# Two blocks on one core: the first two projections interleaved with their splits moved off GpSimd, and the heads' spreads and the mixing weights' loads moved

## The reference

```python
h = concatenate([meta, x])                      # 16 + 1024 tokens, width 1024
u = rmsnorm(h, norm_g)
proj = u @ w_in                                 # 1024 -> 2304 columns
f_in, f_gate, q, k, v, a_gate = split(proj)     # 512, 512, 512, 128, 128, 512
f_out = fourier_branch(f_in, w_fmix, b_fmix) * silu(f_gate)
a_out = attention_branch(rope(rmsnorm(q)), rope(rmsnorm(k)), v) * silu(a_gate)
h = h + concatenate([f_out, a_out]) @ w_out
x = rmsnorm(h, final_g)[:, 16:]
# fourier_branch: real part of a 2D FFT over tokens and 64 channels of a group,
# then a 64 x 64 mix for each of 8 groups, plus b_fmix
... second block: retention and latent attention, gated feed-forward, gated embedding
```

## Time and profile before

| | us |
|---|---|
| median of 3 runs (2277.14 to 2283.83) | 2279.16 |
| the profiled execution | 2278.32 |
| its span | 2276.3 |
| TensorE busy, share of the span | 92% |
| first projection begins | 33.78 |
| projection of v ended | 113.1 |
| gate 7 ended | 290.7 |

### The profile page before, as it was taken

The page is one execution under the profiler, slowest core; times in us unless marked ns, Lnnn a source line. Parts: engine busy times, 40 slices in busy tenths (PEclk is TensorE's granted clock), DMA queues, the critical chain, the costliest instruction groups (busy, mean ns, idle before and its releaser), DMA issues.

```text
span 2276.3 us, 24686 instructions
## 1 busy us (share of the span) xinstructions
PE 2085.4 (92%) x9915; PEld 1718.9 (76%) x9915; DVE 1167.8 (51%) x1592; ACT 703.0 (31%) x1220; POOL 708.5 (31%) x460
## 2 busy tenths in 40 slices
PE   4988998999799999978888798999999999999878
PEld 3976866777687888856776586788888888888667
DVE  5244127999677354455544446444443344444745
ACT  3011125888443223236555444200000000000541
POOL 2332305888100000005556100333343334433020
PEclk9988998999899999989998799999999999999989
DMA  3112100000333111100000222111111111111012
GB/s 136 47 38 78 38 19 1 1 1 1 111 93 131 55 38 37 39 28 19 19 19 19 93 92 65 56 54 49 47 47 48 54 47 47 47 56 65 29 37 93
DMA packets 34304, 113.42 MB, mean 50 GB/s; under 512 B 3664, under 2 KB 5456, under 8 KB 34192
## 3 DMA queue, kind: packets, MB, share of 16 engines
q1 hardware_dynamic: 24336, 88.20, 12.3%
q10 hardware_dynamic: 9856, 23.65, 2.8%
HBM read 103.46 MB, written 8.39 MB: 49 GB/s over the span
## 4 chain that ended last, share of the span: by engine, by line
PE 77%; DVE 11%; ACT 5%; POOL 4%; issue 2%; DMA 1%; ACTq 0%; SPq 0%; POOLq 0%; DVEq 0%
PE psb L316 21%; PE psa L316 20%; PE psd L316 10%; PE psc L316 9%; PE psd L909 2%; PE psd L1829 2%; PE psc L887 1%; PE psc L1792 1%; POOL pb L1046 1%; DVE wl L343 1%; PE psc L356 1%; DVE ptl L1010 1%; DVE tiny L993 1%; POOL qst L844 1%; DVE tiny L1760 1%
## 5 line engine op out<-in xcount | busy, mean ns | idle before, releaser
L327 POOL TENSOR_TENSOR wh<-wraw,one 128x1024 fp32r<-128x1024 f32 x82 | 156.4, 1907 | 756.3 <-PE psc L316 267.7
L330 POOL TENSOR_TENSOR wl<-wraw,wh 128x1024 fp32r<-128x1024 f32 x82 | 198.6, 2422 | 6.4
L316 PE MATMUL psb<-mh,wh 128*128 128x512 f32 x512 | 174.5, 397 | 2.4 <-issue 2.4
L316 PE MATMUL psa<-mh,wh 128*128 128x512 f32 x448 | 158.7, 407 | 17.2 <-ACT mh L1089 14.4
L1781 POOL TENSOR_TENSOR lps<-lps,tiny 128x128 f32<-128x128 f32 (+2 forms) x24 | 14.7, 613 | 511.2 <-DVE tiny L1776 510.6
L316 PE MATMUL psb<-ml,wh 128*128 128x512 f32 x512 | 172.6, 393 | 0.0
L316 PE MATMUL psb<-mh,wl 128*128 128x512 f32 x512 | 172.4, 392 | 0.0
L316 PE MATMUL psa<-ml,wh 128*128 128x512 f32 x448 | 156.0, 401 | 3.2 <-DVE ml L2083 2.7
L316 PE MATMUL psa<-mh,wl 128*128 128x512 f32 x448 | 154.8, 398 | 0.0
L1046 POOL TENSOR_TENSOR pb<-pb,tiny 128x1024 f32<-128x1024 f32 x64 | 121.2, 1894 | 85.8 <-DVE tiny L1004 84.1
L2132 ACT ACTIVATE th<-hf 128x1024 f32<-128x1024 f32 x22 | 23.3, 1061 | 391.4 <-DVE hf L2146 391.4
(11 more groups left out here) (528 smaller groups left out, 5079.6 us busy)
## 6 DMA issues: line engine op xcount, KB each, us to landing
wraw<-slabs SPq DMA_DIRECT2D x160, 512.0 KB, 3.5
x<-xT SPq DMA_DIRECT2D x8, 520.0 KB, 10.2
h<-xT ACTq DMA_DIRECT2D x8, 512.0 KB, 6.3
residual<-h ACTq DMA_DIRECT2D x8, 512.0 KB, 6.7
h<-residual ACTq DMA_DIRECT2D x8, 512.0 KB, 7.6
outT<-h ACTq DMA_DIRECT2D x16, 256.0 KB, 2.1
ct<-dft ACTq DMA_DIRECT2D x1, 1300.0 KB, 5.9
st<-dft ACTq DMA_DIRECT2D x1, 1300.0 KB, 8.8
```

Of the source, the lines that this page charges most:

```text
L316: t = e.matmul(o, lhsT=lw, rhs=xx(kt, c0, cn), start=n == 0, stop=n == total - 1, skip_group_check=True)
L327: e.tensor_tensor(WH[j][:, :], RAW[:, j, :], ONE[:, 0:1].to_broadcast([P, 1024]), MUL).then_inc(*pooled.up(("high", s)))
L330: e.tensor_tensor(WL[j][:, :], RAW[:, j, :], WH[j][:, :], SUB).then_inc(*pooled.up(("split", s)))
```

## The change

1. `act_norm1` computes the root of one constant first, before the squares. Squares go to five work tiles in turn instead of two, and wait for the sum four tiles back.
2. The first four slabs are split by ScalarE and VectorE. GpSimd makes no low part of x.
3. `pe_f_in` interleaves projections 0 and 1: each tile of x goes through both before the next tile. Projections 2 and 3 are done as before; `dve_f_in` puts the low part of slab 2 behind its first output and that of slab 3 behind its second.
4. `pe_head_norm` is cut into sums and spread. The spread of head j now stands one projection later; the gates 0 and 1 are drawn into the heads' functions, so that the spread of head 4 stands behind gate 1 and the mixes behind gate 2. The turned heads alternate between a work tile and the last part of Q1, the sums' and spreads' PSUM pair between C and D.
5. WF and CD have another place in memory, free once x is normalised, and are loaded from there on. CT and ST are loaded after the mixes.

```diff
-            return S_OUT1 + 2 <= s < S_MLA + 3 or S_OUT2 + 2 <= s < S_FFN + 8 or s >= S_PLEP
+            return s < 4 or S_OUT1 + 2 <= s < S_MLA + 3 or S_OUT2 + 2 <= s < S_FFN + 8 or s >= S_PLEP
...
         def act_norm1(e):
...
+            e.wait_ge(*landed["cols"].on("all"))
+            e.activation(TINY[:, 0:1], col("eps"), ACT.Sqrt).then_inc(*acted.up("root table"))
             for kt in range(KT):
                 e.wait_ge(*landed[f"x{kt}"].on("all"))
-                if kt >= 3:
-                    e.wait_ge(*vec.on(("x sum", kt - 2)))
...
+                if kt >= 5:
+                    e.wait_ge(*vec.on(("x sum", kt - 4)))
+                e.activation(x_square(kt), X[:, kt, :], ACT.Square).then_inc(*acted.up(("x sq", kt)))
+            for s in range(2):
+                act_split(e, s)
...
+            load(e, "wf", WF[:, :], wf)
+            load(e, "cd", CD[:, :, :], cd.rearrange("a p c -> p a c"))
+            for s in range(2, 4):
+                act_split(e, s)
...
         def dve_f_in(e):
...
                 t.then_inc(*vec.up(("ft", j)))
+                if j < 2:
+                    dve_split(e, S_IN1 + j + 2)
 
         def pe_f_in(e):
...
+            for kt in range(KT):
+                e.wait_ge(*acted.on(("x high", kt)))
+                for pas in range(3):
+                    if pas == 1:
+                        e.wait_ge(*x_low(kt))
+                    for j in range(2):
+                        w = (WL if pas == 2 else WH)[j][:, kt * P:kt * P + P]
+                        x = (XL if pas == 1 else XH)[:, kt, :]
+                        for o, c0, cn in thirds(*((A, C), (B, Dp))[j]):
+                            t = e.matmul(o, lhsT=w, rhs=x[:, c0:c0 + cn], start=kt == 0 and pas == 0,
+                                         stop=kt == KT - 1 and pas == 2, skip_group_check=True)
...
-        norm_pair = [C, C, Dp, C, Dp]
+        norm_pair = [C, Dp, C, Dp, C]
...
         def pe_heads(e):
...
-            e.wait_ge(*acted.on("v1"))
-            pe_head_norm(e, 0)
             for j in range(1, 5):
...
+                e.wait_ge(*acted.on(("head in", j - 2) if j >= 3 else "v1" if j == 2 else ("head in", 0)))
                 project(e, S_IN1 + 5 + j, full, xh, xl, halves((A, B)[(j - 1) % 2]), ("head", j))
                 if j >= 2:
-                    pe_head_norm(e, j - 1)
+                    pe_head_spread(e, j - 2)
+                pe_head_sums(e, j - 1)
+            pe_gate(e, 0)
+            pe_head_spread(e, 3)
+            pe_head_sums(e, 4)
+            pe_gate(e, 1)
+            pe_head_spread(e, 4)
...
         def dve_heads(e):
             dve_turn(e, 0)
-            dve_head_norm(e, 0)
+            dve_head_rstd(e, 0)
             dve_turn(e, 1)
...
+            for j in range(3):
+                dve_head_out(e, j)
+                dve_head_rstd(e, j + 1)
+                dve_turn(e, j + 2)
+            dve_gate(e, 0)
+            dve_head_out(e, 3)
+            dve_head_rstd(e, 4)
+            dve_gate(e, 1)
+            dve_head_out(e, 4)
...
         def act_fourier_loads(e):
-            e.wait_ge(*vec.on(("heads", 4)))
-            load(e, "wf", WF[:, :], wf)
-            load(e, "cd", CD[:, :, :], cd.rearrange("a p c -> p a c"))
             e.wait_ge(*vec.on("ft folded"))
+            e.wait_ge(*psum.on("mixes"))
...
-            for s in range(2, S_OUT1 + 2):
+            for s in range(4, S_OUT1 + 2):
                 split(e, s)
```

More of the change, by code:

```diff
@@ L484, in dve_norm1 @@
                     e.wait_ge(*vec.on(("x sum", kt - 1)))
-                e.tensor_tensor(TMP[4][:, :], TMP[4][:, :], TMP[kt % 2][:, :], ADD).then_inc(*vec.up(("x sum", kt)))
+                e.tensor_tensor(TMP[4][:, :], TMP[4][:, :], x_square(kt), ADD).then_inc(*vec.up(("x sum", kt)))
+            for s in range(2):
+                dve_split(e, s)
             e.wait_ge(*acted.on("x root"))
@@ L494, in dve_norm1 @@
                                            in1=RS[:, :], op0=MUL, op1=MUL).then_inc(*vec.up(("x norm", m)))
-                if m >= 1 and not low_on_pool(m - 1):
+                if m >= 1:
                     e.wait_ge(*acted.on(("x high", m - 1)))
@@ L502, in pool_norm1 @@
             e.wait_ge(*pooled.on("one"))
[L503 to L509, removed]
         raw1, sqt, t1, rsk, t2 = TMP
@@ L563, in act_head_norm, with pe_head_sums, pe_head_spread @@
                 e.wait_ge(*psum.on(("head spread", j - 1)))
-            token_root(e, pair, HD, 2, ("head root", j), meta=j == 0)
+            token_root(e, pair, HD, 2, ("head root", j), meta=j == 0, bank=j % 2)
             e.wait_ge(*vec.on(("head rstd", j)))
             repeat(e, TOK[:, 0:18], 2, rsk[:, 0:T], ("head repeat", j), meta=j == 0)
-        def pe_head_norm(e, j):
-            pair = norm_pair[j]
+        def pe_head_sums(e, j):
             e.wait_ge(*acted.on(("head sq", j)))
-            if j == 2:
-                e.wait_ge(*vec.on(("heads", 0)))
-            elif j >= 3:
-                e.wait_ge(*vec.on(("heads", j - 2)))
-            elif j == 1:
-                e.wait_ge(*vec.on(("heads", 0)))
-            token_sums(e, pair, sqt, SQC[:, 2, 0:P:HD], 2, ("head sums", j), meta=j == 0)
-            e.wait_ge(*acted.on(("head repeat", j)))
-            spread(e, pair, rsk[:, 0:T], ("head spread", j), meta=Dp if j == 0 else None)
+            if j >= 2:
+                e.wait_ge(*vec.on(("heads", j - 2)))
+            token_sums(e, norm_pair[j], sqt, SQC[:, 2, 0:P:HD], 2, ("head sums", j), meta=j == 0, bank=j % 2)
+        def pe_head_spread(e, j):
+            e.wait_ge(*acted.on(("head repeat", j)))
+            if j == 1:
+                e.wait_ge(*vec.on(("heads", 0)))
+            spread(e, norm_pair[j], rsk[:, 0:T], ("head spread", j), meta=Dp if j == 0 else None)
         def dve_turn(e, j):
             w, g = (L, "k_g") if j == 0 else (T, "q_g")
+            t1 = turned_in(j)
             e.wait_ge(*acted.on(("head in", j)))
```

81 lines of the change are left out of this document (34 added, 47 removed).

## The result

| | before | after |
|---|---|---|
| median of 4 runs each, same chip | 2278.15 | 2247.92 (2244.66 to 2249.41) |
| ratio | | 0.9868 (95%: 0.9854 to 0.9882) |
| profiled execution | 2278.32 | 2247.43 |
| its span | 2276.3 | 2245.6 |
| first product | 33.78 | 29.76 |

The change saves 30.2 us by the medians. The forecast was 2242 in a range of 2236 to 2255: right in sign and range, 6 us too low.

The account below looks back on a forecast made before the run. TensorE, busy 92% of the span, bounds the kernel, losing time only where it waits or runs slowly. 8.2 us gone to the end of v plus 28.2 in heads and gates make 36.4: 2278.3 to 2241.9, forecast 2242, range 2236 to 2255.

Parts of the forecast that it names:

- Until the first product: Start: without GpSimd's split beside the last sum and the late table load, first product at 30.8, 3.0 us gone.
- The first two projections: Projections 0 and 1 interleaved: TensorE becomes the limit, they end at 55.9 instead of 67.5, 11.6 us gone.
- The bubble: Behind projections 0 and 1: TensorE idles 2.3 us for VectorE's slab 2 subtraction, plus 1.1 us for a clock drop.
- The heads and gates: End of v to gate 7: idle gone, spreads and mixes at high clock, 149.4 us against 177.6, 28.2 gone.
- Fourier products and attention follow gate 7 as before and shift as a block: Behind gate 7: unedited stages only start earlier, no change in the time; 3 us either way in the range.
- Rival 1: Heads and gates: the clock falls at each light stretch of sums and spread, time 2254; chance 0.20.
- Rival 2: Heads: VectorE's loop of 14.1 us against TensorE's 13.7 sets the pace, time 2246; chance 0.08.
- Rival 3: Start: slab 1 late or slow clock longer (3 us), or slab 2 late (3 us), time 2248; chance 0.08.
- Rival 4: Denser stretch of heads: TensorE without rest is granted half speed for part of it, time 2314; chance 0.02.

Follow-up runs that it names:

- heads_only: The kernel before with only items 4 and 5 of the change (heads, gates, weight loads), first part as before: 2255.57 us, ratio 0.9902.
- before_again: The kernel before the change, run once more unchanged for a second profile: 2275.93 us, one run.
- seq_proj: The changed kernel without the interleaving, projections 0 and 1 one after the other: 2247.12 us, ratio 0.9866.
- spread_twice: The changed kernel with the eight transposes of each head's spread done twice: 2251.63 us, ratio 0.9886.
- late_weights: The changed kernel with WF and CD loaded behind the heads, shortly before use: 2247.06 us, ratio 0.9870.
- after_again: The changed kernel, run once more unchanged for a second profile: 2245.41 us, one run.
- pad_6: The changed kernel with 6 matmuls of 512 columns, output unread, put ahead of gate 7: 2247.45 us, ratio 0.9874.
- pad_12: The changed kernel with 12 matmuls of 512 columns, output unread, put ahead of gate 7: 2249.24 us, ratio 0.9878.
- sums_twice: The changed kernel with the eight two-column sum matmuls of each head done twice: 2262.82 us, ratio 0.9938.

## Why the prediction was right or wrong

1. **Until the first product: right, size 1 us short.** Forecast 30.8, measured 29.76. The two causes are seen, the sum of 1.25 us and the table load at 2.28. The rest is x, which landed about 1 us earlier than in the profile of before. It is the spread of the start: heads_only and before_again, whose start is that of before, have the first product at 33.2, and the eleven profiles with the changed start at 29.65 to 30.76.
2. **The first two projections: right.** They take 24.7 us against 25.1 forecast, and end at 54.4 instead of 67.5. By seq_proj, of these 13.1 us 4.0 are the earlier first product, 3.2 the faster projection 0 with all low parts on VectorE, 5.9 the interleaving. Half of the 3.2 is luck of the profile that I compared with: before_again ended its second projection at 65.4, not 67.5. The 0.4 by which I missed is of that kind too: the low clock behind the first product, for which I took 4.6 us, lasted 3.5 here and 3.0 to 6.0 in the 14 profiles. What I didn't price is that the bubble is the price of the interleaving alone, which leaves 1.9 of the 5.9.
3. **The bubble: right.** Forecast 2.3, measured 2.27, released by the subtraction named. The clock behind it was low for 3.4 us, 1.7 lost: the upper of my two ends, where I took 1.1. It fell behind seven of the eight such bubbles that were profiled, and not in spread_twice. V ended at 104.1, forecast 104.9: 1.0 and 0.4 us too early by items 1 and 2, 0.6 too late by this one.
4. **The heads and gates: right.** From 104.1 to 255.3 are 151.2 us against 149.4. Spreads took 0.87 (0.83 taken), the mixes 1.91 (1.9), idle none. The projections are 11.24 to 11.34 behind sums where I took 11.14, and the one drop cost 1.6 where I took 0.7. The early loads, which I credited with part of it, are worth nothing (late_weights): with the mixes behind gate 2 their loads are in time anyway. That attribution was wrong, and cost the sum nothing.
5. **"Fourier products and attention follow gate 7 as before and shift as a block": wrong, and this is the miss.** 35.4 us of 36.4 were won up to gate 7; then 5.1 were given back, in stretches that nobody had edited, with 10 us more at the low clock. I had allowed 3 us either way for it in the range and nothing in the time. Without it the time would be 2243, 1 us from the forecast.

Rival 1 (a drop at each light stretch, 2254) came true once in five, behind the first spread, and in after_again, pad_6 and pad_12 not at all; sums_twice shows how near its edge was: eight more sums bring all of them. Rival 2 did not occur: no wait for VectorE between the heads. Rival 3 neither: slab 2's high part was ready, and the bubble was of the expected length. Rival 4 is refuted: 93.4 us without rest had a mean clock of 0.98.

Open is why both profiles of before have the clock fall 1.4 us or more behind the first Fourier product and most profiles of the changed kernels 0.6 to 0.9, and what besides that place makes the later part long or short. Also open is whether a wait placed there could hold the fall at the better place.

## What to carry to other kernels

Before interleaving two producers' consumers, look at where the first output comes free: letting one of the pair run ahead for the last tiles won back the 4.1 us that the plain interleaving wasted. Work moved out of a gap is best moved beside work that keeps TensorE's clock up, and of the small operations here, in the doses tried, the transposes do that and the two-column sums don't. And count a saved microsecond as saved only at the end: on a kernel whose clock changes many times, what is unedited can cost 5 us more or less from one version or execution to the next.

## What the runs showed of the hardware

- Between projections, transposes of 128 columns left the granted clock at 1.00 (eight in 0.87 us, sixteen on end without a drop), while two sets of two-column sums on end, some 3.6 us, let it fall each time.
- The idle 2.43 us ahead of the first Fourier product brought a drop in 12 of 14 profiled executions and none in two, with the same work around it.
- The same addition on VectorE took 2.98 us beside GpSimd's split and 1.25 without it.
- The place of a drop relative to the same instruction differed by 1.2 us between two executions of one kernel (+0.8 and -0.4), and executions of one kernel differed by 5 us.
- The low clock behind the first product lasted 3.0 to 6.0 us in the 14 profiled executions (3.5 and 4.8 in two of one kernel).
- The idle 2.27 us behind the interleaved projections brought a drop of 3.4 us in seven of eight profiled executions.
